# Output products of three layers: tile pairs by seven block products instead of eight, block sums on GpSimd

## The chip, the cores and the metric

One Trainium2 chip, all 8 cores, each with one sequence of the prompt and 16 of the 128 sample sequences. No core talks to another. The metric is the device time of one launch in microseconds, set by the slowest core. The kernel before takes 2015.86 us (median of 3 runs, 2015.81 to 2016.44).

## The reference

A trunk of four layers; each layer normalises its input, projects it, mixes it in three groups of heads, projects the mix back and adds it to the stream:

```
h    = rmsnorm(x, pre_g)
proj = h @ w_in                      # (tokens, 1024) @ (1024, 6400)
u, v, z_a, p, z_b, xc, bg, cg, z_c = split(proj)
a = u * (tril(w_s) @ rmsnorm(v, v_g) + b_s)      # chunks of 128 tokens
b = (pooled mean of p - p) @ w_pg * pool_scale   # windows 2, 4, 8, 16
c = bg * conv3(cg * xc)
mix = concat(a * silu(z_a), b * silu(z_b), c * silu(z_c))   # width 2048
out = mix @ w_out                    # (tokens, 2048) @ (2048, 1024)
x   = x + rmsnorm(out, post_g)
```

The change concerns `out = mix @ w_out` in layers 0, 1 and 2. Layer 3 keeps its form. The next layer's `v` is computed from the new `x` in the same stage, tile by tile.

## The kernel before, in words

A core holds 17 tiles of 128 tokens (tile 16 is the sample group). Activations lie in `big`, 24 slots of 128 channels by 2176 tokens in bf16: 8 slots hold the normalised, transposed input of the current layer (`h0(l)`), 16 hold the mix, and the 8 of the next layer's input are among those 24 in turn. `wout` holds the 16 blocks (128 by 1024) of the layer's output weight in bf16; `ring` holds 8 blocks of input weights, of which `v` takes 6.

For each layer the order is: `b_stage` (pooling), `a_stage` (gating MLP), `c_stage` (convolution), then the output stage, a loop over the tiles in `OUT_ORDER` (16, 0, 1, ... 15). `c_stage` goes over 6 channel blocks; in each it goes over the chunks of tokens in the order 128 (tile 16), 512, 512, 512, 512, and a chunk is four products of 8 matmuls (`mm8`, line 550). At the end of a channel block its four weights are released. That is when GpSimd issues the loads for the slots that came free (lines 481 and 489) and some blocks of `wout` (line 547). At the end of the last channel block of a layer, GpSimd issues the 8 loads of the next `v` weight and two more.

The output stage before, per tile: `out_mm` (line 851) is 16 k-steps by two halves of 512 columns, 32 matmuls into two PSUM banks. `out_ew` squares and sums on ScalarE, `rstd` (line 572) adds epsilon and takes the power -0.5 in two small GpSimd instructions, VectorE scales from PSUM (`stt`) and adds the stream (`tt`), and the tile is stored to `x_mid`. `norm` squares again on ScalarE, uses `rstd` once more, and VectorE writes the next layer's input, which `t_dma` transposes into `big`. Three tiles later `v_mm` multiplies by the `v` weight (16 matmuls) and `v_ew` normalises (ScalarE, `rstd`, VectorE). So a tile needs three `rstd` on GpSimd. Three tiles of `v` are left over at the end of the loop; two of them are placed into the next `b_stage`.

Order: each engine runs its instructions in the order in which they were emitted, and `emit` places the semaphore waits. Where `Plan.on` is set, `emit` collects items instead, and `plan_order` (line 154) then gives out an order: it repeatedly takes the item that could start earliest by the given durations (`dur`) and the dependencies inside the plan, the earlier item on a tie, every engine being free at 0.5. Before, only the start of layer 0 is ordered so; the output stages stand in written order.

## Time and profile before

| | |
|---|---|
| median of 3 runs | 2015.86 us |
| profiled execution, its own time | 2017.03 us |
| its span (slowest core, core 7) | 2015.6 us |
| spans of the 8 cores | 2012.4 to 2015.6 us |
| busy, share of the span | PE 99%, VectorE 54%, ScalarE 29%, GpSimd 18% |
| granted clock of TensorE, mean of the cores | 0.998 to 1.000 of full speed |

"Busy" is the share of the span in which an engine had an instruction under way; loads of matmul weights are counted apart (PEld) and overlap the matmuls. In lists of instructions, "out<-in" are the tiles written and read, and an idle time in brackets is that of the engine before the instruction, with what ended it.

### The profile page before, as it was taken

To read this page: it belongs to the slowest core of one execution; us is meant where nothing else is said; L and a number is where in the kernel's file an instruction comes from. 1 tells how busy PE (TensorE), PEld (TensorE's weight loads), DVE (VectorE), ACT (ScalarE), POOL (GpSimd) and SP (SyncE) were. 2 spreads that over 40 slices of the span, in tenths; PEclk is the share of its full clock that TensorE was granted. 3 is DMA by queue.
4 is the path that set the end of the run, shared out by engine and by line. 5 is a ranking of instruction groups with operands and counts; after the bars stand their busy time and mean duration, and the time that the engine had idled before them with its cause. 6 is when DMAs were issued, how large, how long until landed. Compare 5 with 4: busy or idle time off the path is not lost.

```text
span 2015.6 us, 32819 instructions; the slowest of 8 cores (2012.4 to 2015.6 us)
## 1 busy us (share of the span) xinstructions
PE 1990.4 (99%) x10940; PEld 992.7 (49%) x10940; DVE 1091.0 (54%) x1613; ACT 581.8 (29%) x1127; POOL 367.6 (18%) x701
## 2 busy tenths in 40 slices
PE   6999999999999999999999999999999999999998
PEld 4545554444454554444444555444445455544444
DVE  4675555554575555555457555554545745555433
ACT  4432122223332122223334212222333421222211
POOL 4510011033330001113332001111333100110011
PEclk9999999999999999999999999999999999999999
DMA  8633244384443235518444324443753432353243
GB/s 213 123 58 69 37 89 61 66 199 136 131 84 68 33 63 79 84 29 218 136 121 74 62 43 82 60 74 65 209 134 113 63 76 33 53 81 46 84 147 136
DMA packets 133798, 188.11 MB, mean 93 GB/s; under 512 B 72577, under 2 KB 78977, under 8 KB 133634
## 3 DMA queue, kind: packets, MB, share of 16 engines
q0 software_dynamic: 41040, 71.39, 23.6%
q1 hardware_dynamic: 92450, 114.43, 19.0%
q8 instruction: 92, 1.51, 0.3%
q14 instruction: 72, 0.59, 0.1%
q10 hardware_dynamic: 144, 0.20, 0.0%
HBM read 199.26 MB, written 42.35 MB: 120 GB/s over the span
## 4 chain that ended last, share of the span: by engine, by line
PE 98%; DMA 1%; DVE 0%; issue 0%; POOL 0%; ACT 0%; SPq 0%; POOLq 0%; DVEq 0%; ACTq 0%
PE ps L553 64%; PE ps L855 23%; PE ps L618 9%; PE ps L759 1%; DMA sb_wout<-w_v 1%; PE ps L731 1%; PE ps L890 0%; DMA sb_ar<-x_in 0%; POOL sb_stats L576 0%; DVE sb_hbuf L538 0%; PE ps L602 0%; DVE sb_big L608 0%; ACT sb_hbuf L529 0%; DVE sb_ar L923 0%; DVE sb_big L538 0%
## 5 line engine op out<-in xcount | busy, mean ns | idle before, releaser
L553 PE MATMUL ps<-sb_big,sb_ring 128*128 128x512 bf16 (+2 forms) x7104 | 1327.4, 346 | 3.5 <-DVE sb_big L608 2.2
L553 PEld LDWEIGHTS ps<-sb_big,sb_ring 128*128 128x128 bf16 x7104 | 634.2, 98 | 640.7 <-issue 4.8
L529 ACT ACTIVATE sb_ar<-ps 128x512 f32<-128x512 f32 (+3 forms) x511 | 302.8, 594 | 881.8 <-PE ps L553 549.3
L855 PE MATMUL ps<-sb_wout,sb_big 128*128 128x512 bf16 x2144 | 469.8, 379 | 0.0
L855 PEld LDWEIGHTS ps<-sb_wout,sb_big 128*128 128x128 bf16 x2144 | 209.8, 98 | 248.8
L481 POOL DMA_DIRECT2D sb_ring<-w_t x176 | 94.0, 541 | 925.3 <-PE ps L553 464.2
L534 DVE TENSOR_TENSOR sb_ar<-ps,sb_ar 128x512 f32<-128x512 f32 (+2 forms) x243 | 146.2, 602 | 161.4 <-PE ps L553 157.4
L538 DVE SCALAR_TENSOR_TENSOR sb_ar<-ps,sb_stats,sb_post_bc 128x1024 f32<-128x1024 f32 x67 | 86.0, 1284 | 209.1 <-POOL sb_stats L576 208.5
L538 DVE SCALAR_TENSOR_TENSOR sb_ar<-sb_pcx,sb_convw,sb_ar 128x512 f32<-128x512 f32 (+1 forms) x196 | 145.1, 740 | 88.9 <-ACT sb_ar L815 78.7
L534 DVE TENSOR_TENSOR sb_pcx<-ps,sb_ar 128x512 f32<-128x512 f32 (+1 forms) x98 | 66.7, 681 | 203.8 <-PE ps L553 203.8
L576 POOL TENSOR_TENSOR sb_stats<-sb_stats,sb_neghalf 128x1 f32<-128x1 f32 x203 | 161.0, 793 | 30.1 <-POOL sb_stats L574 0.3
L534 DVE TENSOR_TENSOR sb_big<-sb_ar 128x512 bf16<-128x512 f32 (+2 forms) x242 | 147.4, 609 | 26.0 <-DVE sb_ar L534 0.9
L574 POOL TENSOR_SCALAR sb_stats<-sb_stats 128x1 f32<-128x1 f32 x203 | 52.4, 258 | 513.1 <-ACT sb_ar L529 293.4
L618 PE MATMUL ps<-sb_ring,sb_big 128*128 128x512 bf16 (+1 forms) x816 | 140.4, 326 | 0.0
L815 ACT ACTIVATE sb_ar<-sb_pcx,sb_convw 128x512 f32<-128x512 f32 (+1 forms) x98 | 69.8, 712 | 194.6 <-DVE sb_pcx L534 191.2
L538 DVE SCALAR_TENSOR_TENSOR sb_hbuf<-sb_ar,sb_stats,sb_pre_bc 128x1024 bf16<-128x1024 f32 x53 | 68.1, 1285 | 75.6 <-POOL sb_stats L576 74.2
L618 PEld LDWEIGHTS ps<-sb_ring,sb_big 128*128 128x128 bf16 x816 | 79.7, 98 | 57.2
L534 DVE TENSOR_TENSOR sb_ar<-sb_ar 128x1024 f32<-128x1024 f32 (+4 forms) x91 | 90.8, 997 | 10.1 <-DVE sb_ar L534 0.7
L529 ACT ACTIVATE sb_hbuf<-sb_ar 128x1024 bf16<-128x1024 f32 x53 | 56.0, 1057 | 121.9 <-DVE sb_ar L534 116.0
L538 DVE SCALAR_TENSOR_TENSOR sb_big<-ps,sb_stats,sb_vb_bc 128x768 bf16<-128x768 f32 x64 | 65.1, 1017 | 37.2 <-POOL sb_stats L576 33.2
L529 ACT ACTIVATE sb_big<-ps 128x768 bf16<-128x768 f32 x68 | 55.0, 808 | 83.0 <-PE ps L618 80.6
L534 DVE TENSOR_TENSOR sb_ar<-ps,sb_vb_bc 128x512 f32<-128x512 f32 (+1 forms) x120 | 72.1, 601 | 0.0
(89 smaller groups left out, 636.5 us busy)
## 6 DMA issues: line engine op xcount, KB each, us to landing
sb_ring<-w_t POOLq DMA_DIRECT2D x176, 256.0 KB, 5.3
x_mid<-sb_ar SPq DMA_DIRECT2D x51, 512.0 KB, 2.7
sb_ar<-x_mid SPq DMA_DIRECT2D x51, 512.0 KB, 4.0
sb_wout<-w_out POOLq DMA_DIRECT2D x64, 256.0 KB, 9.0
sb_ar<-x_in SPq DMA_DIRECT2D x20, 512.0 KB, 3.9
y_o<-sb_ar SPq DMA_DIRECT2D x16, 512.0 KB, 2.9
sb_big<-x_in SPq DMA_DIRECT2D x9, 512.0 KB, 9.3
sb_ring<-w_v POOLq DMA_DIRECT2D x24, 192.0 KB, 12.2
```

Source lines behind the costliest of these rows:

```text
L481: emit(POOL, lambda g: g.dma_start(out=flat, in_=a.src), reads=a.gate, writes=a.res, dsem=d_ring[pos], dur=0.58)
L529: return emit(ACT, lambda a: a.activation(out=out, in_=in_, func=func, scale=scale, **kw), reads=reads, writes=writes, dur=0.17 + elems(in ...
L534: return emit(DVE, lambda v: v.tensor_tensor(out=out, in0=in0, in1=in1, op=op), reads=reads, writes=writes, dur=0.15 + elems(out) / 950)
L538: return emit(DVE, lambda v: v.scalar_tensor_tensor(out=out, in0=in0, scalar=scalar, in1=in1, op0=op0, op1=op1), reads=reads, writes=write ...
L553: ins = pe.matmul(bank(b, n), lhsT=wa.ap[:, k, :], rhs=big[:, h0(l) + k, c0:c0 + n], start=(k == 0), stop=(k == 7))
L574: emit(POOL, lambda g: g.tensor_scalar(out=col, in0=col, scalar1=EPS, scalar2=None, op0=ALU.add), reads=[R_stat[si]], writes=[R_stat[si]], ...
L576: emit(POOL, lambda g: g.tensor_tensor(out=col, in0=col, in1=neghalf[:], op=ALU.pow), reads=[R_stat[si], R["neghalf"]], writes=[R_stat[si] ...
L618: ins = pe.matmul(bank(b + bo, n), lhsT=big[:, s0 + k, j * 128:(j + 1) * 128], rhs=wv.ap[:, k, c0:c0 + n], start=(k == 0), stop=(k == 7))
L731: emit(PE, lambda pe: pe.matmul(bank(b, n), lhsT=wpg[:, gi, :], rhs=dd, start=True, stop=True), reads=rm + [R["wpg"]], writes=[bank_res[b]])
L759: ins = pe.matmul(ps[:, 512 * b + jj * 128:512 * b + (jj + 1) * 128], lhsT=big[:, 16 + h, c0 + jj * 128:c0 + (jj + 1) * 128], rhs=wsrc[:, ...
L815: emit(ACT, lambda a_: a_.activation(out=yv, in_=taps[0], func=AF.Copy, scale=cw[:, 0:1]), reads=list(rd) + [R["convw"]], writes=[R_ar[y]] ...
L855: ins = pe.matmul(bank(b + half), lhsT=mix_ap(l, k, j * 128, 128), rhs=wout[:, k, half * 512:(half + 1) * 512], start=(k == 0), stop=(k == ...
```

## The change

The mix of two neighbouring tiles is taken as a 2 by 2 matrix of blocks (tile j or j+1; k-steps 0 to 7 or 8 to 15) and the output weight as another (k-steps; column half). Seven products of 8 matmuls each (56) replace eight (64), by Winograd's form: four sums of mix blocks and four of weight blocks go in, and seven additions put the products together. Three tiles (16, 0, 1) keep the old form, seven pairs (2,3) to (14,15) take the new one.

- `weight_sums`: three sums of weight blocks, each 8 by 512 columns wide, in four GpSimd instructions of 128x1024 bf16, so 12 in a layer. They stand in `c_stage`, after chunks 1, 2 and 3 of the last channel block, ahead of the release of its weights, and write into columns of the layer's input that are no longer read (sum 0 into tiles 0 to 3, sum 1 into tiles 4 to 7, sum 2 into tiles 8 to 11).
- `last_weight_sum`: the fourth, in place in `wout`, on VectorE in four instructions of 128x1024 bf16, after the three single tiles.
- `pair_sums`: four GpSimd instructions of 128x1024 bf16 for each pair, 28 in a layer; those of the first pair are emitted right behind the product of tile 16 and ahead of its `done`.
- `pair_mm`: seven products into banks 0 to 5; a ScalarE copy of 128x512, three VectorE additions of bank and buffer into a buffer (`usum`), four into the bank (`padd`).
- `place`: the order of the 16 blocks in `wout` matches the slots of the mix; `R_wout` has one entry for each half block.
- The output stage of layers 0 to 2 is ordered by `plan_order`. Two of the tiles of `v` come behind the plan, two go into the next `b_stage` as before. The out-stage's temporary is one buffer (8, 9) instead of two in turn.

```diff
+SEVEN = (0, 1, 2)
+LONE = (16, 0, 1)
...
+        def ptt(out, in0, in1, op, reads, writes):
+            return emit(POOL, lambda g: g.tensor_tensor(out=out, in0=in0, in1=in1, op=op),
+                        reads=reads, writes=writes, dur=0.2 + elems(out) / 480)
+
+        def weight_sums(l, i):
+            for k0 in range(0, 8, 2):
...
+                ptt(T_ap(l, i, k0, 2), ins[0], sec[0], ALU.subtract, ins[1] + sec[1], T_res(l, i, k0, 2))
...
                 for ci in (4, 0, 1, 2, 3):
                     c_chunk(l, c, wts, *CHUNKS[ci])
+                    if c == 5 and l in SEVEN and ci in (1, 2, 3):
+                        weight_sums(l, ci - 1)
                 for a in wts:
                     release(a)
...
+        def pair_sums(l, j, S):
+            a11, a12, a21, a22 = A_of(l, 0, j), A_of(l, 1, j), A_of(l, 0, j + 1), A_of(l, 1, j + 1)
+            s1, s2, s4 = (S_of(l, i) for i in S)
+            for o, x, y, op in ((s1, a21, a22, ALU.add), (s2, s1, a11, ALU.subtract), (s4, a12, s2, ALU.subtract),
+                                (a21, a11, a21, ALU.subtract)):
+                ptt(o[0], x[0], y[0], op, x[1] + y[1], o[1])
...
+        def pair_mm(l, j, S, between_):
+            s1, s2, s4 = (S_of(l, i) for i in S)
+            prod(A_of(l, 0, j), B_of(0, 0), 4)
+            act(U_ap[0], bank(4), AF.Copy, reads=[bank_res[4]], writes=[U_res[0]])
+            prod(s2, T_of(l, 1), 5)
+            usum(1, 0, 5)
+            prod(s1, T_of(l, 0), 3)
+            usum(2, 1, 3)
+            prod(s4, B_of(1, 1), 1)
+            padd(1, 2)
+            prod(A_of(l, 1, j), B_of(1, 0), 0)
+            padd(0, 0)
+            between_()
+            prod(A_of(l, 0, j + 1), B_of(0, 1), 4)
+            usum(1, 1, 4)
+            padd(3, 1)
+            prod(A_of(l, 1, j + 1), T_of(l, 2), 2)
+            padd(2, 1)
...
+                for i, j in enumerate(LONE):
+                    b = 2 * (i % 2)
+                    out_mm(l, j, b)
+                    if i == 0:
+                        pair_sums(l, 2, sets[0])
+                        sp_dma(samp[:], sp_in[l + 1], [], [R["samp"]], d_c["samp"])
+                    done(j, b)
+                    x_ahead(i + 4)
+                last_weight_sum()
+                for p in range(7):
+                    j = 2 * p + 2
+
+                    def mid(j=j, p=p):
+                        done(j, 0)
+                        x_ahead(j + 5)
+                        if p < 6:
+                            pair_sums(l, j + 2, sets[p + 1])
+                        next_v()
+                    pair_mm(l, j, sets[p], mid)
+                    done(j + 1, 2)
+                    x_ahead(j + 6)
+                    if p < 6:
+                        next_v()
```

## Rows read from the trace of the kernel before

**Rows 1.** The page: span, busy times, granted clock in 40 slices.
```profile
span 2015.6 us, 32819 instructions; the slowest of 8 cores (2012.4 to 2015.6 us)
...
PE 1990.4 (99%) x10940; PEld 992.7 (49%) x10940; DVE 1091.0 (54%) x1613; ACT 581.8 (29%) x1127; POOL 367.6 (18%) x701
...
PEclk9999999999999999999999999999999999999999
```

**Rows 2.** The page: the chain that ended last, by line.
```profile
PE ps L553 64%; PE ps L855 23%; PE ps L618 9%; PE ps L759 1%; DMA sb_wout<-w_v 1%; PE ps L731 1%; PE ps L890 0%; DMA sb_ar<-x_in 0%; POOL sb_stats L576 0%; DVE sb_hbuf L538 0%; PE ps L602 0%; DVE sb_big L608 0%; ACT sb_hbuf L529 0%; DVE sb_ar L923 0%; DVE sb_big L538 0%
```

**Rows 3.** Chain in order of time, output stage of layer 0: start us, us, what.
```profile
407.81 27.63 PE ps L855 x128
...
438.04 6.91 PE ps L855 x32
444.94 2.60 PE ps L618 x16
...
559.02 5.20 PE ps L618 x32
564.23 3.45 PE ps L553 x16
567.68 2.60 PE ps L618 x16
570.28 2.17 PE ps L553 x16
572.45 2.60 PE ps L618 x16
575.05 3.45 PE ps L553 x16
```

**Rows 4.** Busy time by engine, output stage of layer 0: us, then busy (x instructions).
```profile
407.60:568.00 160.40, 160.40 (x804) 78.57 (x803) 81.98 (x70) 51.86 (x99) 57.00 (x108) 1.00 0.57 155
```

**Rows 5.** Timeline of GpSimd, start of that stage: start us, us, instruction.
```profile
408.66 4.33 POOL L489 DMA_DIRECT2D sb_ring<-w_v  x8 [54.38 <-PE ps L553]
412.92 1.12 POOL L481 DMA_DIRECT2D sb_ring<-w_t  x2
416.15 0.22 POOL L574 TENSOR_SCALAR sb_stats<-sb_stats 128x1 f32<-128x1 f32 x1 [2.11 <-ACT sb_ar L529]
416.52 0.57 POOL L576 TENSOR_TENSOR sb_stats<-sb_stats,sb_neghalf 128x1 f32<-128x1 f32 x1
```

**Rows 6.** GpSimd's instructions, shapes kept apart: xcount, busy us, mean ns.
```profile
L920 POOL TENSOR_TENSOR sb_ar<-sb_ar 128x192 f32<-128x192 f32 x1 | 0.6, 587 | 0.1
...
L905 POOL TENSOR_TENSOR sb_stats<-sb_stats 128x1 f32<-128x1 f32 x1 | 0.2, 189 | 1.1 <-ACT sb_hbuf L529 1.1
```

**Rows 7.** Timeline at 476 us, VectorE and GpSimd.
```profile
476.00 1.28 DVE L538 SCALAR_TENSOR_TENSOR sb_ar<-ps,sb_stats,sb_post_bc 128x1024 f32<-128x1024 f32 x1 [3.01 <-POOL sb_stats L576]
...
477.38 1.23 DVE L534 TENSOR_TENSOR sb_ar<-sb_ar 128x1024 f32<-128x1024 f32 x1
477.64 1.39 POOL L576 TENSOR_TENSOR sb_stats<-sb_stats,sb_neghalf 128x1 f32<-128x1 f32 x1
```

**Rows 8.** VectorE's instructions, shapes kept apart: xcount, busy us, mean ns, idle before.
```profile
L538 DVE SCALAR_TENSOR_TENSOR sb_ar<-sb_pcx,sb_convw,sb_ar 128x512 f32<-128x512 f32 x188 | 141.3, 751 | 88.0 <-ACT sb_ar L815 78.2
L534 DVE TENSOR_TENSOR sb_big<-sb_ar 128x512 bf16<-128x512 f32 x190 | 131.6, 693 | 20.5 <-DVE sb_ar L534 0.9
L534 DVE TENSOR_TENSOR sb_ar<-ps,sb_ar 128x512 f32<-128x512 f32 x190 | 130.7, 688 | 158.4 <-PE ps L553 154.3 <-PE ps L759 4.0
L538 DVE SCALAR_TENSOR_TENSOR sb_ar<-ps,sb_stats,sb_post_bc 128x1024 f32<-128x1024 f32 x67 | 86.0, 1284 | 209.1 <-POOL sb_stats L576 208.5 <-ACT sb_big L529 0.6
L534 DVE TENSOR_TENSOR sb_ar<-sb_ar 128x1024 f32<-128x1024 f32 x67 | 82.2, 1226 | 7.4 <-DVE sb_ar L538 0.5
L538 DVE SCALAR_TENSOR_TENSOR sb_hbuf<-sb_ar,sb_stats,sb_pre_bc 128x1024 bf16<-128x1024 f32 x53 | 68.1, 1285 | 75.6 <-POOL sb_stats L576 74.2 <-POOL sb_stats L574 1.4
L538 DVE SCALAR_TENSOR_TENSOR sb_big<-ps,sb_stats,sb_vb_bc 128x768 bf16<-128x768 f32 x64 | 65.1, 1017 | 37.2 <-POOL sb_stats L576 33.2 <-PE ps L618 4.0
...
L534 DVE TENSOR_TENSOR sb_bdt<-sb_bdt,sb_cstb 128x768 bf16<-128x768 bf16 x4 | 2.2, 551 | 0.0
...
L534 DVE TENSOR_TENSOR sb_ar<-ps,sb_post_bc 128x768 f32<-128x768 f32 x1 | 1.0, 957 | 1.2 <-ACT sb_hbuf L529 1.2
```

**Rows 9.** ScalarE's instructions, shapes kept apart.
```profile
L529 ACT ACTIVATE sb_ar<-ps 128x512 f32<-128x512 f32 x348 | 207.2, 596 | 579.6 <-PE ps L553 527.1 <-DVE sb_big L534 46.0 <-PE ps L731 6.5
L529 ACT ACTIVATE sb_ar<-ps 128x1024 bf16<-128x1024 f32 x67 | 68.5, 1022 | 235.7 <-PE ps L855 235.0 <-POOL sb_stats L574 0.7
...
L529 ACT ACTIVATION_READ_ACCUMULATOR sb_ar<-ps 128x1 f32 x67 | 13.0, 194 | 0.0
```

More of the change, by code:

```diff
@@ L656, in mask_small, with place, wout_piece @@
             tt(bdt[:], bdt[:], m, ALU.mult, [R["bdt"], R["cstb"]], [R["bdt"]])
-        def wout_piece(l, k):
-            pool_dma(wout[:, k, :], w_out[l, k * 128:(k + 1) * 128, :], [R_wout[k]], d_wout[k])
+        def place(l, k):
+            if l not in SEVEN:
+                return k
+            s_ = mslot(l, k)
+            return s_ - 8 + h0(l) if s_ < 16 else s_ - 8
+        def wout_piece(l, kk):
+            k = [place(l, i) for i in range(16)].index(kk)
+            pool_dma(wout[:, kk, :], w_out[l, k * 128:(k + 1) * 128, :], R_wout[2 * kk:2 * kk + 2], d_wout[kk])
@@ new lines, in B_ap, with B_res, T_ap, T_res @@
+        def B_ap(half, ch, k0=0, n=8):
+            return wout[:, 8 * half + k0:8 * half + k0 + n, ch * 512:(ch + 1) * 512]
+        def B_res(half, ch, k0=0, n=8):
+            return [R_wout[2 * (8 * half + k) + ch] for k in range(k0, k0 + n)]
+        def T_ap(l, i, k0=0, n=8):
+            return big[:, h0(l) + k0:h0(l) + k0 + n, i * 512:(i + 1) * 512]
+        def T_res(l, i, k0=0, n=8):
+            return [R_big[h0(l) + k][4 * i + t] for k in range(k0, k0 + n) for t in range(4)]
+        def T_of(l, i):
+            return T_ap(l, i), T_res(l, i)
@@ L661, in b_stage, with last_weight_sum @@
+        def last_weight_sum():
+            for k0 in range(0, 8, 2):
+                tt(B_ap(0, 1, k0, 2), B_ap(1, 1, k0, 2), B_ap(0, 1, k0, 2), ALU.subtract,
+                   B_res(0, 1, k0, 2) + B_res(1, 1, k0, 2), B_res(0, 1, k0, 2))
         def b_stage(l, between):
```

68 lines of the change are left out of this document (63 added, 5 removed).

## The prediction

> **What bounds the kernel now.** I read the page's head first: TensorE has work under way in 99% of the span, at the granted clock 9 tenths or more in every slice, and GpSimd is busy in 18% [rows 1]. Then the chain that ended last: 96% of it is matmuls of lines 553, 855 and 618, and no other engine has more than 1% [rows 2]. So a matmul that goes gives its time back, until something else becomes late. The chain in order of time shows the stage that is changed. One tile's output product is 32 matmuls in 6.91 us (0.216 us each), one tile's `v` product 2.60 us, and they follow each other without a gap [rows 3]. In that stage VectorE is busy 82 of 160 us and GpSimd 57 [rows 4]. The reader should see that TensorE has no slack and that the others have about half, and ask whether the added work fits into that half at each place, not on the mean.
>
> **Matmuls removed.** A pair takes 56 in place of 64: 8 x 0.216 = 1.73 us [rows 3]. With 7 pairs and 3 layers that is 36.3 us, 12.1 in a layer. The `v` products and the weight loads per matmul stay.
>
> **The price of one GpSimd sum.** No row shows one of 128x1024 bf16. The two rows of a plain tensor_tensor on GpSimd give 0.189 us for 1 column and 0.587 for 192 [rows 6], so 2.08 ns a column, and 0.19 + 1023 x 0.00208 = 2.32 us for 1024. Those rows are f32. On VectorE a bf16 sum of 768 columns took 0.551 us against 0.957 for an f32 one out of PSUM [rows 8]; the same factor of 0.58 would give 1.34 us here, which is my lower bound. I take 2.32, since it is from GpSimd itself, and 2.42 with about 0.1 us between instructions, as between the two VectorE instructions at 476.00 and 477.38 [rows 7]. The upper bound is 2.42 plus a wait for VectorE, which comes next.
>
> **GpSimd is held by VectorE.** The power on GpSimd takes 0.57 us by itself [rows 5], but 1.39 us when it starts while VectorE adds two SBUF tiles: it ended at 479.03, 0.42 us after VectorE's end at 478.61 [rows 7]. In two output stages that I went through, all but one of the powers that met this addition were stretched so. The VectorE instructions with two SBUF inputs are the addition of the stream (1.23 us) and the scaling in `norm` (1.29) in each tile, and in a chunk of `c_stage` two of 0.75 and one of 0.69, together 2.2 us [rows 8]. Whether GpSimd's long sums hold VectorE in turn, no row shows: from 0 to 2.3 us for each such instruction. I take little of it and keep the rest as a rival.
>
> The Trainium skill ("SBUF — State Buffer", section "Who interferes with whom") says that VectorE with two SBUF inputs and a GpSimd instruction that reads SBUF exclude each other: whoever comes first keeps the shared port for the whole instruction. By that rule VectorE is held too; the trace agrees for the direction that it shows (0.57 against 1.39 us).
>
> **Start of the output stage.** Let 0 be the end of the last chunk of `c_stage` on TensorE (407.81 in layer 0) [rows 3]. The first weight sum overwrites columns that chunk 0 of the last channel block reads, so it starts when chunk 0 is done, three chunks before 0. A chunk is 32 matmuls, 6.91 us, so at -20.7. GpSimd has nothing to do then (54.38 us idle before 408.66) [rows 5]. The 12 sums take 29.0 us. VectorE has 2.2 us of instructions with two SBUF inputs per chunk, some 7 us over this stretch; GpSimd loses from 0 to 7, I take 5. So the weight sums end at +13.3 (bounds +8.3 and +15.3). Behind them in GpSimd's queue are the eight loads of the `v` weight and two others, 5.4 us from 408.66 to 414.04 [rows 5]: +18.7. Then come the planned items. The planner takes GpSimd as free at 0.5, though it is not, and the first pair's four sums depend on nothing in the plan: at 2.33 + 0.08 each they are set from 0.5 to 10.1. The `rstd` of tile 16 can start by its durations only at about 9.0 (matmuls to 7.4, square and sum 1.2, two hand-overs of 0.2), where the fourth sum is already under way. So all four sums stand ahead of the first `rstd`: +18.7 + 9.7 = +28.4. `rstd` takes 0.9 us (416.15 to 417.09) [rows 5], VectorE's scaling 1.28 [rows 8], with hand-overs +31. Only then are banks 0 and 1 free for tile 1. TensorE has done tiles 16 and 0 by 13.8 and waits for them, 17 us. Without any holding by VectorE it would wait 12. All the matmul time that a layer saves, 12.1 us, goes here already; net +5 us a layer.
>
> In the queue behind are the other `rstd`, and nothing else can go in TensorE's place, since the planner sees that bank free at 12.8 and puts tile 1 next. The `v` weights are issued 13 us later than before; their first use comes 29 us after 0 without the stall, and later with it, so they aren't late.
>
> **The pairs.** TensorE needs 56 x 0.216 + 2 x 2.60 = 17.3 us a pair, against 19.0 for the two tiles before. GpSimd needs four sums, 9.7, and six `rstd` of about 1.0 us with the gap, 6.0, so 15.7 us without being held. VectorE's four instructions with two SBUF inputs are 5.0 us a pair, so from 15.7 to 20.7; since GpSimd is nearly always at work it meets most of them, and I take 0.7 of it: 19.2. VectorE itself: 2 x (1.28 + 1.23 + 1.29 + 1.02) = 9.6 [rows 8], and seven additions of 128x512. Four of these write to PSUM, which no row shows; the nearest is 0.688 for PSUM and SBUF to SBUF, the bounds are 0.6 and 1.3 (half and all of a 1024-column instruction), and I take 0.69: 4.8. With 15 gaps of 0.1 it is 15.9 of 17.3 us. So there is little room: the cover that hid everything before is used up, and GpSimd sets the pace at 19.2. It is 1.9 us a pair above TensorE's need, in six pairs 11, less some 3 us by which GpSimd gets ahead while TensorE does tile 1: +8 us a layer.
>
> **At nothing.** The ScalarE copy (0.6 us a pair [rows 9]; ScalarE is busy a third of the stage [rows 4]). `last_weight_sum`: four bf16 sums, by 0.551 x 1024/768 about 0.73 each, 3 us behind tile 1; its product comes 8.6 us later. Uncovered it would be 3 us a layer. The single temporary: its user comes every 8 us and holds it some 5; if GpSimd is late, it is late by the same wait. The order of `wout` changes no count of loads. SP's loads and stores are the same number, in a planned order, with buffers four tiles deep. At the end of the stage tile 15 has one addition more, 0.7 us, on a chain that had 16.0 us from 559.02 to chunk 3 at 575.05 [rows 3] and needs about 11; a GpSimd that is late by over 4 us there would cost the difference, 0 to 3 us a layer, taken as 0.
>
> **Sum.** In a layer +5 + 8 = +13, in three +39. Against the profiled execution's own 2017.0 (span 2015.6) this is 2056; the median of the runs is 1.2 lower, so 2055 us.
>
> **Rivals.**
> (a) GpSimd's bf16 sums are short, 1.34 us, and the change wins. The weight sums then end about at 0 (the last four can't start before -6.9), the loads at +6.3, the pair's sums at +12, bank 0 is free at +14.6, a stall of 1 us. A pair costs GpSimd 5.8 + 6.0 + at most 5.0 = 16.8 < 17.3. Each layer gains 11, in all 34 us: 1982. For it speaks VectorE's gain in bf16, against it that nothing of the kind is seen on GpSimd. It decides from about 1.8 us a sum down.
> (b) The sums are as long as I take them, but being held costs little, since GpSimd's waits fall where it is idle anyway. The stall of 12 us eats the gain and the pairs run at TensorE's pace: 2016, no change.
> (c) The two engines hold each other. VectorE's 15.9 us a pair get up to 4 waits of some 1.5 us, 22 us a pair: 4.7 over TensorE's need, in six pairs 28 less 3. In `c_stage` VectorE falls behind as well and the stall grows to 20. In a layer +8 + 25 = 33, minus overlap of the two some 3: 2016 + 90 = 2106. For it: both engines are nearly full. By the rule of the Trainium skill named above ("SBUF — State Buffer", "Who interferes with whom") this one would hold; no row bears out the half that decides.
> The fix in (a) could also come from the planned order being other than I worked out (an `rstd` ahead of the sums): then the stall shrinks by up to 9.7 us a layer, and the pairs' pace decides; that lies between (a) and (b).
>
> **Chances.** My forecast 0.44, (a) with its relatives 0.29, (b) 0.09, (c) 0.18. The forecast's own range is 2030 to 2080, from the bounds of the holding. The whole range leaves out the fastest part of (a) (0.09) and the slower half of (c) (0.1): 1982 to 2096. A measurement of this kernel can tell about 0.2% (4 us) from no change. Faster by more 0.29; within it 0.07; slower 0.64.
>
> **What would show it.** GpSimd's sums in the trace: 2.3 us each, longer beside VectorE's additions (steps on price and holding), or 1.3. GpSimd's queue at the start of the stage: weight sums until after the end of `c_stage`, ten loads, four sums, and only then line 574. TensorE idle of 12 to 20 us before the third tile, ended by VectorE's scaling. In the pairs: TensorE idle in each, of 1 to 3 us, and 19 us from pair to pair. The three output stages 163 to 166 us long in place of 151 (plus the last `v` products). If the third tile follows without a gap, the start step is wrong; if the pairs take 17.3 us, the step on the pairs is. The prediction is wrong as a whole if the sums take under 1.8 us.

## The result and the profile after

The changed kernel takes 2082.16 us (median of 4 runs) against 2016.15 us for the kernel before beside it: ratio 1.0321, 95% interval 1.0305 to 1.0336. It is slower by 66 us. The forecast was 2055 us; its own range, 2030 to 2080, ends 2 us below the measured time, and the whole range, 1982 to 2096, holds it. In some of the runs below the cores of one die ran at a lower clock, so beside each time stands the span of a core that was not concerned.

The page of the changed kernel: span, busy time by engine, granted clock and the chain that ended last.

```profile
span 2079.6 us, 32826 instructions; the slowest of 8 cores (2077.2 to 2079.6 us)
...
PE 1970.1 (95%) x10567; PEld 978.2 (47%) x10772; DVE 1262.1 (61%) x1772; ACT 589.5 (28%) x1148; POOL 646.6 (31%) x821
...
PEclk9999999989999999999999999999999999999999
...
PE 79%; POOL 8%; issue 6%; DVE 4%; DMA 2%; ACT 1%; POOLq 0%; DVEq 0%; SPq 0%; ACTq 0%
```

The chain by engine, in the page of the kernel before:

```profile
PE 98%; DMA 1%; DVE 0%; issue 0%; POOL 0%; ACT 0%; SPq 0%; POOLq 0%; DVEq 0%; ACTq 0%
```

TensorE's busy time fell by 20 us, its share of the chain from 98% to 79%, and GpSimd's busy time grew by 279 us. GpSimd has 8% of the chain now and VectorE 4%. The sums' own durations are in the list of GpSimd's instructions (xcount, busy us, mean ns of one, idle before):

```profile
L697 POOL TENSOR_TENSOR sb_big<-sb_big 128x1024 bf16<-128x1024 bf16 x84 | 191.7, 2287 | 17.3 <-PE ps L922 14.9 <-POOL sb_big L697 1.5
...
L697 POOL TENSOR_TENSOR sb_big<-sb_wout,sb_big 128x1024 bf16<-128x1024 bf16 x24 | 58.1, 2455 | 0.0
L697 POOL TENSOR_TENSOR sb_big<-sb_wout 128x1024 bf16<-128x1024 bf16 x12 | 30.1, 2533 | 102.3 <-PE ps L555 102.3
```

The pair sums have a median of 2.12 us (2.10 at the least, 3.11 at the most), where 2.32 was worked out from the f32 rows of 1 and 192 columns [rows 6]. The weight sums have a median of 2.57. The factor of 0.58 that VectorE's bf16 row gave doesn't appear on GpSimd; an f32 sum of this size was not run there.

The start of the output stage of layer 0, GpSimd's timeline (start us, us, instruction, idle before):

```profile
386.81 9.71 POOL L697 TENSOR_TENSOR sb_big<-sb_wout 128x1024 bf16<-128x1024 bf16 x4 [32.97 <-PE ps L555]
396.48 19.38 POOL L697 TENSOR_TENSOR sb_big<-sb_wout,sb_big 128x1024 bf16<-128x1024 bf16 x8
415.80 4.28 POOL L491 DMA_DIRECT2D sb_ring<-w_v  x8
420.00 1.13 POOL L483 DMA_DIRECT2D sb_ring<-w_t  x2
421.06 2.21 POOL L697 TENSOR_TENSOR sb_big<-sb_big 128x1024 bf16<-128x1024 bf16 x1
423.54 2.12 POOL L697 TENSOR_TENSOR sb_big<-sb_big 128x1024 bf16<-128x1024 bf16 x1 [0.26 <-POOL sb_big L697]
425.86 4.20 POOL L697 TENSOR_TENSOR sb_big<-sb_big 128x1024 bf16<-128x1024 bf16 x2 [0.20 <-POOL sb_big L697]
430.15 0.22 POOL L576 TENSOR_SCALAR sb_stats<-sb_stats 128x1 f32<-128x1 f32 x1
```

and TensorE's, in layer 0 and in layer 1:

```profile
407.21 7.07 PE L909 MATMUL ps<-sb_wout,sb_big 128*128 128x512 bf16 x31
418.01 10.00 PE L909 MATMUL ps<-sb_wout,sb_big 128*128 128x512 bf16 x32 [3.73 <-DVE sb_ar L536]
432.87 3.57 PE L909 MATMUL ps<-sb_wout,sb_big 128*128 128x512 bf16 x8 [4.86 <-DVE sb_ar L540]
...
923.52 13.98 PE L909 MATMUL ps<-sb_wout,sb_big 128*128 128x512 bf16 x63
949.71 8.70 PE L909 MATMUL ps<-sb_wout,sb_big 128*128 128x512 bf16 x31 [12.21 <-DVE sb_ar L540]
```

This is the queue that was forecast, in its order: 12 weight sums from -20.4 us (the stage starts at 407.2), ten loads, four sums, and only then the first `rstd`, at +22.9. The third tile's product waits for VectorE's scaling of the first.

The two engines hold each other. That VectorE holds GpSimd shows in the weight sums of `c_stage`, which take 2.57 us where VectorE works beside them and 2.12 otherwise. That GpSimd holds VectorE is in the timeline of VectorE in the last channel block, where GpSimd runs sums without a pause from 386.81 on:

```profile
386.78 5.22 DVE L540 SCALAR_TENSOR_TENSOR sb_ar<-sb_pcx,sb_convw,sb_ar 128x512 f32<-128x512 f32 x2 [0.92 <-ACT sb_ar L867]
...
400.30 1.82 DVE L536 TENSOR_TENSOR sb_big<-sb_ar 128x512 bf16<-128x512 f32 x1
402.05 2.08 DVE L854 COPY sb_pcx<-sb_pcx 128x2 f32<-128x2 f32 x1
404.24 0.69 DVE L536 TENSOR_TENSOR sb_pcx<-ps,sb_ar 128x512 f32<-128x512 f32 x1
```

Two instructions that took 0.75 us each before take 5.22 together, the one of 0.69 us takes 1.82 [rows 8]. The addition that reads PSUM and one SBUF tile keeps its 0.69.

**Where the 64 us are.** The table reads four points of the output stage from TensorE's timeline, in us from the stage's first product, median of the three layers: the start of the second product of the first pair, the end of the last output product, the first product of the next `b_stage`, and the first matmul with `wpg` in it, which all kernels reach behind the same work.

| kernel | time, us | span of a core, us | pairs from | products to | b_stage | wpg |
|---|---|---|---|---|---|---|
| before | 2016.2 | 2015.6 | | 151.4 | 156.4 | 170.7 |
| the change | 2082.2 | 2079.6 | 36.5 | 162.7 | 172.7 | 192.1 |
| planner told, rstd first | 2130.8 | 2097.1 | 24.2 | 166.7 | 179.3 | 197.1 |
| weight sums on VectorE | 2069.8 | 2053.7 | 28.5 | 154.6 | 163.0 | 184.1 |
| no pair sums | 2058.0 | 2026.5 | 27.6 | 145.2 | 155.4 | 174.7 |
| no post-additions | 2075.7 | 2067.1 | 36.4 | 163.7 | 168.7 | 187.9 |
| all sums on VectorE | 2083.6 | 2037.0 | 22.5 | 150.2 | 157.1 | 178.9 |
| pair sums split two and two | 2094.0 | 2064.0 | 29.3 | 156.6 | 169.0 | 187.9 |
| other banks at the end | 2139.1 | 2083.7 | 36.9 | 162.8 | 168.6 | 194.0 |
| five pairs, interleaved | 2036.0 | 2032.1 | 15.8 | 144.4 | 160.7 | 175.0 |
| same, banks and order | 2007.7 | 2006.2 | 15.5 | 146.1 | 153.1 | 167.4 |
| six pairs | 2010.4 | 2008.5 | 15.5 | 144.9 | 152.7 | 168.6 |
| seven pairs in a row | 2066.8 | 2038.5 | 22.5 | 147.0 | 153.2 | 178.4 |
| five pairs, tile sums on GpSimd | 2043.9 | 2039.2 | 15.5 | 158.1 | 165.1 | 179.4 |

The change loses 192.1 - 170.7 = 21.4 us a layer, 64.2 in three, which is the whole difference of the spans (64.0). By TensorE's need it should have gained 12.1, so 33.5 us a layer are to be placed. Start: 36.5 less three tiles (20.7) and a product (1.7), 14.1. Pairs: 126.2 from 36.5 to 162.7, against 116.8 for 48 products of 8 matmuls (83.0) and 13 `v` products (33.8), 9.4. End: 162.7 to 192.1 is 29.4 against 19.3 before, 10.1. In sum 33.6.

### The profile page after: what moved, and what is told of

The parts are those of the page before. It is cut to its first block, busy times and chain, and to the rows that moved or that the text cites. A ratio compares the mean times of both kernels' runs of the same rounds, so it can differ in the third digit from the quotient of the medians.

```text
span 2079.6 us, 32826 instructions; the slowest of 8 cores (2077.2 to 2079.6 us)
## 1 busy us (share of the span) xinstructions
PE 1970.1 (95%) x10567; PEld 978.2 (47%) x10772; DVE 1262.1 (61%) x1772; ACT 589.5 (28%) x1148; POOL 646.6 (31%) x821
## 4 chain that ended last, share of the span: by engine, by line
PE 79%; POOL 8%; issue 6%; DVE 4%; DMA 2%; ACT 1%; POOLq 0%; DVEq 0%; SPq 0%; ACTq 0%
PE ps L555 61%; PE ps L909 6%; PE ps L620 6%; PE ps L922 4%; POOL sb_big L697 4%; POOL sb_stats L578 2%; DVE sb_ar L540 1%; DVE sb_ar L536 1%; PE ps L811 1%; POOL sb_stats L576 1%; PE ps L783 1%; DMA sb_wout<-w_v 1%; POOL sb_ring L491 1%; ACT sb_hbuf L531 1%; DVE sb_big L540 1%
## 5 line engine op out<-in xcount | busy, mean ns | idle before, releaser
L531 ACT ACTIVATE sb_ar<-ps 128x512 f32<-128x512 f32 (+3 forms) x532 | 314.4, 593 | 814.3 <-PE ps L555 531.8
L540 DVE SCALAR_TENSOR_TENSOR sb_ar<-sb_pcx,sb_convw,sb_ar 128x512 f32<-128x512 f32 (+1 forms) x196 | 172.5, 880 | 88.7 <-ACT sb_ar L867 78.5
L909 PE MATMUL ps<-sb_wout,sb_big 128*128 128x512 bf16 x784 | 181.2, 391 | 34.0 <-DVE sb_ar L540 29.3
L697 POOL TENSOR_TENSOR sb_big<-sb_big 128x1024 bf16<-128x1024 bf16 x84 | 191.7, 2287 | 17.3 <-PE ps L922 14.9
L576 POOL TENSOR_SCALAR sb_stats<-sb_stats 128x1 f32<-128x1 f32 x203 | 68.2, 336 | 340.9 <-ACT sb_ar L531 161.0
L536 DVE TENSOR_TENSOR sb_big<-sb_ar 128x512 bf16<-128x512 f32 (+2 forms) x242 | 157.6, 651 | 26.3 <-DVE sb_ar L536 1.4
L922 PE MATMUL ps<-sb_wout,sb_big 128*128 128x512 bf16 x660 | 154.0, 379 | 14.4 <-DVE sb_ar L536 5.8
L578 POOL TENSOR_TENSOR sb_stats<-sb_stats,sb_neghalf 128x1 f32<-128x1 f32 x203 | 145.4, 717 | 29.2 <-POOL sb_stats L576 0.2
L909 PEld LDWEIGHTS ps<-sb_wout,sb_big 128*128 128x128 bf16 x800 | 80.0, 100 | 134.6 <-issue 45.9
L922 PE MATMUL ps<-sb_big 128*128 128x512 bf16 x492 | 114.0, 379 | 4.7 <-DVE sb_ar L540 3.6
L540 DVE SCALAR_TENSOR_TENSOR sb_hbuf<-sb_ar,sb_stats,sb_pre_bc 128x1024 bf16<-128x1024 f32 x53 | 77.9, 1470 | 59.2 <-POOL sb_stats L578 57.9
L922 PEld LDWEIGHTS ps<-sb_wout,sb_big 128*128 128x128 bf16 x672 | 64.3, 98 | 94.1 <-issue 23.0
```

The source lines that it names most:

```text
L531: return emit(ACT, lambda a: a.activation(out=out, in_=in_, func=func, scale=scale, **kw), reads=reads, writes=writes, dur=0.17 + elems(in ...
L536: return emit(DVE, lambda v: v.tensor_tensor(out=out, in0=in0, in1=in1, op=op), reads=reads, writes=writes, dur=0.15 + elems(out) / 950)
L540: return emit(DVE, lambda v: v.scalar_tensor_tensor(out=out, in0=in0, scalar=scalar, in1=in1, op0=op0, op1=op1), reads=reads, writes=write ...
L576: emit(POOL, lambda g: g.tensor_scalar(out=col, in0=col, scalar1=EPS, scalar2=None, op0=ALU.add), reads=[R_stat[si]], writes=[R_stat[si]], ...
L578: emit(POOL, lambda g: g.tensor_tensor(out=col, in0=col, in1=neghalf[:], op=ALU.pow), reads=[R_stat[si], R["neghalf"]], writes=[R_stat[si] ...
L697: return emit(POOL, lambda g: g.tensor_tensor(out=out, in0=in0, in1=in1, op=op), reads=reads, writes=writes, dur=0.2 + elems(out) / 480)
```

## The experiments

**The order at the start.** The planner is told when GpSimd is free, and the first pair's sums come behind the first tile's `rstd`.

```diff
-                s = max(ready, free.get(id(q), 0.5))
+                s = max(ready, free.get(id(q), Plan.late.get(id(q), 0.5)))
...
+                Plan.late = {id(POOL): 14.0}
...
                     if i == 0:
-                        pair_sums(l, 2, sets[0])
                         sp_dma(samp[:], sp_in[l + 1], [], [R["samp"]], d_c["samp"])
                     done(j, b)
+                    if i == 0:
+                        pair_sums(l, 2, sets[0])
```

> The change, but the planner is told that GpSimd is free only at 14 us, and the first pair's four sums are emitted behind the first tile's rstd, not ahead of it. In the change the third tile begins 25.2 us after the end of c_stage and TensorE waits 12.2 us for it. Theory Q (GpSimd's total work and the mutual holding with VectorE set the pace of the whole stage): the wait before the third tile falls from 12 us to about 3, but the four sums are then late for the first pair and the time is given back; the stage gets 0 to 3 us shorter, in all 2072 to 2082 us. Rival O (a wrong order at one place costs its own time and nothing else): 9 us a layer less, 2055 us.

Measured: 2130.8 us, span 2097.1. The pairs begin 12.3 us earlier in the stage, and the stage is still 5 us longer. Both expectations are too low; that the time is given back is theory Q's direction. One place where it is given back can be seen on TensorE in layer 0:

```profile
431.91 1.89 PE L923 MATMUL ps<-sb_big 128*128 128x512 bf16 x8
441.03 3.36 PE L621 MATMUL ps<-sb_ring,sb_big 128*128 128x512 bf16 x10 [7.23 <-issue]
```

No engine releases the first `v` product at 441.03. Its weights were not late: the last of them landed at 435.96, 5 us before. What landed last is the transposed copy of tile 16 that the product reads: issued at 431.29, landed at 440.01, 1.0 us before the product. In layer 1 it is the same: the weights at 955.40, the copy at 960.32, the product at 961.33 after a wait of 3.34 us. The copy took 8.7 us in layer 0, where 2.8 is usual; the ten loads moved beside it, which is a likely reason and was not tested. Why the pairs are slower too (142.5 us in place of 126.2) is not settled.

**Weight sums on VectorE.**

```diff
-                ptt(T_ap(l, i, k0, 2), ins[0], sec[0], ALU.subtract, ...
+                tt(T_ap(l, i, k0, 2), ins[0], sec[0], ALU.subtract, ...
```

> The change with its 12 weight sums a layer on VectorE in place of GpSimd. GpSimd then has nothing in c_stage; VectorE gets 12 bf16 instructions of 0.68 us (last_weight_sum's unhindered duration), 9.4 us with gaps, where it had 8.4 us idle in three chunks. Theory Q: the loads of the v weight go out at once, the first pair's sums end at +14, the third tile's wait falls to 2 or 3 us; the pairs keep their pace of 18.7 us (12.4 us above TensorE's need in 7 pairs): each layer gets 10 us shorter, 2050 us. Rival V (VectorE's load is what limits, GpSimd's is not): VectorE is late by what it takes on, gain under 4 us a layer, 2070 us or more.

Measured: span 2053.7 (2069.8 as timed). 26 us in all less than the change, 8.1 a layer at `wpg`; of this the start has 8.0, and the pairs keep their pace (126.1 against 126.2). Theory Q. In `c_stage` four such sums that took 9.71 us on GpSimd take 2.49 on VectorE.

**No pair sums**: the four sums of each pair are left out, so the tiles' outputs are not the reference's.

```diff
-                ptt(o[0], x[0], y[0], op, x[1] + y[1], o[1])
+                pass
```

> The change without its four pair sums a pair on GpSimd (the products take what lies in the buffers; the weight sums stay). Theory Q: with 28 x 2.2 us a layer gone, nothing holds VectorE in the pairs, they run at TensorE's 17.3 us (118.5 us for seven pairs with their v products in place of 130.9), the third tile starts 9 us earlier, and the end of the stage loses its 7 us: about 25 us a layer less, 2005 us. Rival V (VectorE's seven additions a pair set the pace): only the 9 us at the start go, the pairs stay at 18.7: 2053 us.

Measured: span 2026.5; 17.4 us a layer less. The pairs run in 117.6 us, 0.8 over TensorE's need, as theory Q has it, so the seven additions a pair on VectorE, without the sums, hold up nothing in the pairs. The total is neither's, 2005 nor 2053: the end costs what it did in the change, 29.5 us, which neither expected. With theory Q's 7 us less there it would have been about 2005. So the end's cost doesn't come from GpSimd's pair sums.

**No post-additions**: the seven additions of a pair are left out (the products stay uncombined).

```diff
-            tt(U_ap[o], U_ap[a], bank(b), ALU.add, [U_res[a], bank_res[b]], [U_res[o]])
+            pass
...
-            tt(bank(b), bank(b), U_ap[a], ALU.add, [bank_res[b], U_res[a]], [bank_res[b]])
+            pass
```

> The change without the seven additions of 128x512 a pair on VectorE (the products stay uncombined). Theory Q (GpSimd's queue with its holding sets the pace, VectorE is full besides): VectorE has 5.5 us a pair less, meets GpSimd's sums with the same four instructions, and GpSimd's need of 15.7 us plus holds stays: the pairs get a third to a half of their 12.4 us back, the start keeps its 13.8 us: 5 us a layer, 2065 us. Rival V: the pairs run at TensorE's pace and the end of the stage is in time, 19 us a layer less, 2025 us.

Measured: span 2067.1, near the 2065 of theory Q, but from another place. The stage is 4.2 us a layer shorter. The pairs took 127.3 us, 1.1 more than with the additions; the end took 5.2 less (24.2 in place of 29.4). So relieving VectorE buys nothing in the pairs while the GpSimd sums are there. The busy times of the stretch of the pairs, from a window of each kernel (us, then busy PE, PEld, DVE, ACT, POOL), first the change:

```profile
443.80:570.00 126.20, 118.27 (x581) 56.70 (x591) 102.13 (x103) 44.80 (x86) 90.70 (x101) 1.00 0.47 140
```

then the one without post-additions:

```profile
442.90:570.00 127.10, 117.35 (x582) 57.11 (x592) 84.69 (x60) 45.75 (x90) 97.44 (x103) 1.00 0.53 144
```

Neither engine is full: VectorE 81% and GpSimd 72% in the change, 67% and 77% without the additions. Theory Q was right that the loss hangs on the sums, but not by its sum of durations. What TensorE waits for in the pairs are PSUM banks, as in these rows of the change:

```profile
469.66 2.76 PE L620 MATMUL ps<-sb_ring,sb_big 128*128 128x512 bf16 x16 [1.00 <-DVE sb_big L540]
...
479.75 1.89 PE L922 MATMUL ps<-sb_wout,sb_big 128*128 128x512 bf16 x8 [2.15 <-DVE sb_ar L536]
```

A bank goes back through ScalarE, `rstd` on GpSimd and VectorE. With a 2.1 us sum ahead of `rstd` and one more hold on VectorE, that chain can be longer than the two or three products that TensorE has in the meantime. This is a reading of the rows: no run changes the chain's length alone.

**All sums on VectorE.**

```diff
-                ptt(T_ap(l, i, k0, 2), ins[0], sec[0], ALU.subtract, ins[1] + sec[1], T_res(l, i, k0, 2))
+                tt(T_ap(l, i, k0, 2), ins[0], sec[0], ALU.subtract, ins[1] + sec[1], T_res(l, i, k0, 2))
...
-                ptt(o[0], x[0], y[0], op, x[1] + y[1], o[1])
+                tt(o[0], x[0], y[0], op, x[1] + y[1], o[1])
```

> The change with all its sums, of weights and of tiles, on VectorE; GpSimd has the small rstd instructions and its loads alone, as before the change. Theory Q (GpSimd's queue of 2.1 us sums sets the pace, and holding between the two engines makes it worse): no long GpSimd instruction is left; VectorE's need per pair is 15.9 + 4 x 0.78 = 19.0 us, 1.7 above TensorE's; no wait at the start; the end stays at 10 us and the next b_stage at 19.4: some 5 us a layer above the kernel before, 2031 us. Rival V (VectorE's load was the limit already): it gets 12.5 us of sums a layer in c_stage and 22 in the pairs on top, and the time rises above the 2080 of the change.

Measured: span 2037.0, as theory Q (2031) more than rival V. The start is as good as free (22.5 is three tiles and a product). The pairs take 127.7 us, no better than in the change: VectorE is busy 107 of 127.6 us of them. That its own queue now returns the banks late is what this suggests; no run shows it by itself.

**Pair sums split two and two**, with the weight sums on VectorE as well.

```diff
-                ptt(T_ap(l, i, k0, 2), ins[0], sec[0], ALU.subtract, ins[1] + sec[1], T_res(l, i, k0, 2))
+                tt(T_ap(l, i, k0, 2), ins[0], sec[0], ALU.subtract, ins[1] + sec[1], T_res(l, i, k0, 2))
...
-                ptt(o[0], x[0], y[0], op, x[1] + y[1], o[1])
+                (tt if o is s4 or o is a21 else ptt)(o[0], x[0], y[0], op, x[1] + y[1], o[1])
```

> The weight sums on VectorE; of the four sums of a pair two on VectorE (the third and the one in place), two on GpSimd. By needs without holding: VectorE 17.5 us, GpSimd 10.4, TensorE 17.3 a pair. Theory Q: what holding is left comes from two GpSimd sums a pair and costs under 1 us each; pairs near 18 us, no long wait at the start, the end as in the change: 2020 to 2030 us, faster than all sums on VectorE. Rival H (holding by any long GpSimd sum is dear, since VectorE is full): slower than all on VectorE, 2035 to 2050.

Measured: span 2064.0, slower than all on VectorE by 27 us and beyond rival H's upper end. By loads it was the best balanced kernel. The pairs are alike (127.3 us against 127.7); of the 27 us the start has 6.8 a layer and the end 2.6. At the start GpSimd has the four sums of the first two pairs in its queue, from 413.82 to 423.4, and the first `rstd` comes behind them at 423.49. So what the split costs is again a place in GpSimd's queue at the start, not the pace of the pairs.

**Other banks at the end.**

```diff
-                st["bank"] = 0
-                vjob(vq[0])
                 st["bank"] = 4
+                vjob(vq[0])
+                st["bank"] = 0
                 vjob(vq[1])
...
+                def first(j=vq[2]):
+                    st["bank"] = 4
+                    vjob(j)
...
                 def fin(j=vq[3], l=l):
+                    st["bank"] = 0
                     vjob(j)
```

> The change with other PSUM banks for the four v products behind the plan: the first gets banks 4 and 5 (free early), the second 0 and 1, the third 4 and 5, the fourth 0 and 1; in the change the first waits 3.2 us for the scaling of tile 14 out of banks 0 and 1, and the third 3.5 us for the first one's banks. Theory B (the wait is for the bank alone): both waits go, with them most of the lowered clock behind them: 6 to 8 us a layer, 2060 us. Rival C (the last two tiles end 3.5 us apart instead of 9.5, and their elementwise work is late whatever the bank): the waits move to the next product that needs a bank or a transposed tile, 2075 to 2080.

Measured: span 2083.7, rival C (2075 to 2080, a little more). The first wait shrinks from 3.2 to 0.6 us and the third `v` product waits 7.8 instead of 3.5:

```profile
572.16 2.76 PE L620 MATMUL ps<-sb_ring,sb_big 128*128 128x512 bf16 x15 [0.57 <-DVE sb_ar L540]
574.76 3.62 PE L555 MATMUL ps<-sb_big,sb_ring 128*128 128x512 bf16 x16
586.17 4.97 PE L620 MATMUL ps<-sb_ring,sb_big 128*128 128x512 bf16 x16 [7.79 <-DVE sb_big L540]
```

But the third `v` product again gets the banks of the first, now 4 and 5, and waits until VectorE has released them. So the run moves the wait and doesn't answer whether banks of its own for each leftover `v` product would remove it.

**Five pairs between single tiles.** All sums on VectorE. The fourth weight sum goes into freed columns of the layer's input and into `samp`, so that single tiles can still use the whole weight; its product is then 16 matmuls of 256 columns.

```diff
+UNITS = ((16,), (0,), (1, 2), (3,), (4, 5), (6,), (7, 8), (9,), (10, 11), (12,), (13, 14), (15,))
...
+                    if len(u) == 1:
...
+                        out_mm(l, u[0], b)
+                        done(u[0], b)
...
+                    else:
+                        pair_mm(l, u[0], S3, lambda j=u[0]: done(j, 0))
```

> Five pairs instead of seven, each between single tiles: 16, 0, (1,2), 3, (4,5), 6, (7,8), 9, (10,11), 12, (13,14), 15. All sums on VectorE; the fourth weight sum gets a place of its own, so that single tiles can follow pairs. TensorE's need falls by 5 x 1.73 = 8.6 us a layer against the kernel before. Theory Q: with no long GpSimd instruction, what counts is whether VectorE fits; a pair and a single tile need 19.0 + 5.3 of TensorE's 26.8 us, so it fits, the last tile stands alone as before and the end costs what it did before: 26 us gained, 1990 us, up to 2000 if the start is late by VectorE's weight sums. Rival C (products of a pair end too close together for its elementwise chain, wherever it stands): each pair costs its 1.7 us gain again, 2016 us or more.

Measured: 2036.0, span 2032.1. By the total it is rival C (2016 or more). By the products it is nearer to theory Q: they end at 144.4, 7.0 us earlier than in the kernel before, where theory Q had 8.6. But the end costs 30.6 us (144.4 to 175.0), though a single tile is the last unit. There the next 32 `v` matmuls wait 5.3 us and take 7.56, where 5.36 is usual:

```profile
549.32 2.76 PE L620 MATMUL ps<-sb_ring,sb_big 128*128 128x512 bf16 x15
557.38 7.56 PE L620 MATMUL ps<-sb_ring,sb_big 128*128 128x512 bf16 x32 [5.29 <-DVE sb_big L540]
```

The two `v` products in a row both use banks 6 and 7. That, tile 0's bank, and a VectorE sum that waited 4.4 us for a store were mended next.

**The same with banks and order mended**, and **six pairs**.

```diff
-                        v_mm(l + 1, v, 6)
-                        v_ew(l + 1, v, 6)
+                        vb = 4 if nv[0] == 14 else 6
+                        v_mm(l + 1, v, vb)
+                        v_ew(l + 1, v, vb)
...
-                        b = 2 if ui == 1 else 0
+                        b = 6 if ui == 1 else 0
                         out_mm(l, u[0], b)
+                        if ui == 0:
+                            pair_sums(l, pairs_left.pop(0)[0], S3)
                         done(u[0], b)
                         if ui == 0:
                             last_weight_sum(l)
-                            pair_sums(l, pairs_left.pop(0)[0], S3)
...
-                st["bank"] = 4
+                st["bank"] = 2
                 vjob(vq[0])
+                st["bank"] = 6
```

Six pairs differ from it in one line:

```diff
+UNITS = ((16,), (0,), (1, 2), (3, 4), (5,), (6, 7), (8, 9), (10,), (11, 12), (13, 14), (15,))
```

> The interleaved kernel with five pairs, and three places mended that its trace showed idle: the last planned v product and the one behind the plan get banks 4, 5 and 2, 3 in place of 6, 7 and 4, 5 (a 5.3 us wait, and the halved clock behind it); tile 0 gets banks 6 and 7 in place of 2 and 3, which the first pair's second product waited for (1.5 to 5.3 us); and the part of the fourth weight sum that waits 4.4 us for a store stands behind the first pair's sums on VectorE, not ahead of them. Theory Q: with no idle stretch left TensorE's own need decides, 8.6 us a layer under the kernel before: 1990 us, 1998 if the end stays 2 us late. Rival C (pairs bring VectorE's chain late wherever they stand): the waits move on, 2015 or more.

> The same with six pairs: 16, 0, (1,2), (3,4), 5, (6,7), (8,9), 10, (11,12), (13,14), 15. TensorE's need is 10.4 us a layer under the kernel before. Two pairs and a single tile need 2 x 19.0 + 5.3 = 43.3 us of VectorE against 2 x 17.3 + 9.5 = 44.1 of TensorE. Theory Q: it just fits, 1985 us, or VectorE is late where two pairs follow each other (one set of buffers for the tile sums, 1 to 2 us each) and it comes out level with five pairs, 1988 to 1996. Rival C: 2020 us or more.

Measured with five pairs: 2007.7 us, ratio to the kernel before 0.9955, interval 0.9942 to 0.9969: faster than both kernels, by 0.45% over the one before. It lies between theory Q (1990) and rival C (2015), with a third of the gain of theory Q. The end costs 21.3 us in place of 30.6, by banks and order alone. `wpg` is reached at 167.4 in place of 170.7, so 3.3 us a layer are kept of 8.6; the rest is in short waits, among them one in front of the first product of the next `b_stage`:

```profile
560.40 3.61 PE L555 MATMUL ps<-sb_big,sb_ring 128*128 128x512 bf16 x16 [1.77 <-DVE sb_big L540]
```

With six pairs it is 2010.4 us (0.9973, 0.9961 to 0.9984), outside both expectations and 2.7 us slower than five. Its waits in layer 0 are 0.9 us each at the `v` products at the end of the first and the second pair, 1.2 behind the last pair and 2.6 in front of `b_stage`; where the middle pairs meet there is none. So it isn't shown that pairs in a row are what costs the 2.7 us.

**Seven pairs in a row**, else as in the five-pair kernel, but for the banks of the single tiles and of the first leftover `v` product.

```diff
+UNITS = ((16,), (0,), (1,)) + tuple((j, j + 1) for j in range(2, 16, 2))
...
-                        b = 6 if ui == 1 else 0
+                        b = (0, 6, 2)[ui]
...
-                st["bank"] = 2
+                st["bank"] = 0
                 vjob(vq[0])
```

> The last five-pair kernel, 2007.7 us, with the tiles in the order of the change: 16, 0, 1 alone, then seven pairs with no single tile between them. All sums on VectorE, the fourth weight sum in its place of its own. Theory L (each pair hands its elementwise work to engines that must give PSUM banks back within two or three products; a single tile after each pair is what lets them): with VectorE 84% busy the pairs run 1.6 us over TensorE's need as they did with all sums on VectorE, and the last two tiles end close together: 2030 to 2038 us. Rival N (what helped was the banks and the order of the weight sums, and more pairs are better): 12.1 us a layer less matmul time, 1995 to 2002 us.

Measured: span 2038.5, half a microsecond above theory L's upper end. The products end at 147.0, hardly later than with five pairs, but the end costs 31.4 us (147.0 to 178.4) against 21.3, with one wait of 7.5 to 7.9 us in each layer. In layer 0 it is the wait of tile 14's `v` product, which was given banks 0 and 1, held by tile 13's until 571.05. Its other input, tile 14's transposed copy, had landed at 565.71, so of the 7.9 us about 5.3 go to the bank and 2.4 to the tile. Whether a pair as the last unit costs the 10 us, or the banks do, this run doesn't separate; with a single tile last and unlucky banks the end had cost 30.6.

**Five pairs with the tile sums on GpSimd.** (In the five-pair kernel `ptt` issues on VectorE.)

```diff
-                ptt(o[0], x[0], y[0], op, x[1] + y[1], o[1])
+                emit(POOL, lambda g, o=o, x=x, y=y, op=op: g.tensor_tensor(out=o[0], in0=x[0], in1=y[0], op=op),
+                     reads=x[1] + y[1], writes=o[1], dur=0.2 + elems(o[0]) / 480)
```

> The last five-pair kernel, 2007.7 us, with its four tile sums a pair back on GpSimd (the weight sums stay on VectorE). In the 26.8 us of a pair and a single tile GpSimd then has 4 x 2.2 + 9 x 1.0 = 17.8 us, VectorE 3.1 less than its 24. So by load both have more room than in any kernel of the study but the one before. Theory H (what is dear is the small rstd behind a 2.1 us sum and the holding of VectorE, not the load): the banks come back late after each pair, 2 to 4 us each, and the first pair's sums are late behind the loads of the v weight: 2025 to 2050 us. Rival Load (room by the sums of durations is enough): at or below 2007 us.

Measured: 2043.9 us (1.0132, 1.0112 to 1.0152), theory H: 36 us slower than with the same sums on VectorE, though VectorE has 20 bf16 instructions a layer less. One window over the same 119 us of layer 0 (columns as above), first the sums on VectorE:

```profile
430.00:549.00 119.00, 116.69 (x629) 60.79 (x627) 93.32 (x103) 43.37 (x86) 43.21 (x80) 1.00 0.57 161
```

then on GpSimd:

```profile
430.00:549.00 119.00, 109.23 (x572) 55.50 (x570) 87.44 (x83) 38.38 (x75) 75.02 (x87) 0.99 0.54 154
```

VectorE at 73% and GpSimd at 63% keep TensorE waiting; VectorE at 78% and GpSimd at 36% do not. Nothing else differs between the two kernels, so the busy share doesn't decide. The longest waits stand in the first two units with sums, 1.5, 2.5 and 2.9 us:

```profile
433.92 2.76 PE L620 MATMUL ps<-sb_ring,sb_big 128*128 128x512 bf16 x16 [1.50 <-DVE sb_ar L536]
...
441.31 7.07 PE L930 MATMUL ps<-sb_wout,sb_big 128*128 128x512 bf16 x32 [2.46 <-DVE sb_ar L540]
...
457.32 5.30 PE L943 MATMUL ps<-sb_wout,sb_big 128*128 128x512 bf16 x16 [2.89 <-DVE sb_ar L540]
```

More than half of the 12 us that the pairs lose in layer 0 is there, where the first sums stand behind the ten loads; each wait behind is 0.3 to 1.9 us, less than the 2 to 4 that were expected after every pair.

## Why the prediction was right, and where it was off

The direction and the main mechanism were right: the change is slower, because GpSimd's sums stand in the way of its short instructions. The size was nearly right partly by luck. Without the end, which the sum left out, the terms as measured would give about 2051 us; the end, 30 us in all, carried the time out of the forecast's own range.

**Matmuls removed, 12.1 us a layer: right.** With nothing in the way the pairs take 117.6 us (no pair sums) against a need of 116.8.

**The price of one sum, 2.32 us: right in kind**, 2.12 measured, and rival (a), 1.34 us by analogy with VectorE's bf16, was wrong. An operation's own f32 rows on the same engine were the better ground than another engine's gain.

**The start, 17 us: right in mechanism, measured 14.1.** Weight sums ended at +8.6 us (forecast +13.3), the loads at +13.8 (18.7), the four sums at +22.9 (28.4). GpSimd lost about 4 us to holding there, where 5 was taken: nine of the 12 weight sums took 2.57 us and not 2.12. The rest of the difference is the sum itself, which is shorter. In layers 1 and 2 the stall is one wait of 12.2 us before the third tile, the 12 that the prediction gave without any holding, and about 2 us because that tile then takes 8.70 us at a granted clock of 0.81; a slower clock after a wait was no term of the prediction. Only in layer 0 is it different: the row of 3.73 us at the second tile is TensorE waiting for a bank of `c_stage` that VectorE reached late. Rival (c) had this, the forecast did not. Moving only the weight sums away gave back 8.0 us a layer, at this place.

**The pairs, +8 us: right size (9.4), reason in part wrong.** The step set GpSimd's need, 15.7 to 20.7 us a pair, against TensorE's 17.3, as if the fuller engine gave the pace, and had 19.2 us from pair to pair. Measured are 18.3, with waits of 0.3 to 2.2 us, with GpSimd at 72 to 77% and VectorE at 67 to 81%. Without the sums the loss is gone; without VectorE's additions it stays; with the sums on VectorE it stays too. With sums on VectorE and single tiles in between it is nearly gone, and with the same sums on GpSimd it is back, though VectorE has less to do then. That the length of the chain that returns a bank counts, and not the load, fits all of these, but is argued and not shown by a run of its own.

**The end, taken as 0 with 3 us as its bound: this term was wrong.** It measured 10.1 us a layer, 30 of the 66. The step compared one tile's chain, 11 us, with 16.0 us of room. It left out that the last additions complete tiles 14 and 15 only 2.3 us apart (at 568.5 and 570.8 in layer 0), where the products of the last two tiles ended 9.5 us apart before. So two chains stand in the queues of VectorE and ScalarE at once. ScalarE takes its work in the written order, and the leftover `v` products wait behind it. TensorE in layer 0:

```profile
573.17 7.04 PE L620 MATMUL ps<-sb_ring,sb_big 128*128 128x512 bf16 x31 [3.17 <-DVE sb_ar L540]
...
587.18 4.44 PE L620 MATMUL ps<-sb_ring,sb_big 128*128 128x512 bf16 x16 [3.52 <-DVE sb_big L540]
```

and ScalarE, the norm of the last tile and behind it the square of the first of these `v` products, whose matmuls had been done for over 5 us:

```profile
581.72 1.06 ACT L531 ACTIVATE sb_hbuf<-sb_ar 128x1024 bf16<-128x1024 f32 x1 [5.18 <-DVE sb_ar L536]
...
582.78 0.79 ACT L531 ACTIVATE sb_big<-ps 128x768 bf16<-128x768 f32 x1
```

The third `v` product waits for the banks of the first. The end costs 21.3 us with five pairs and mended banks, and 29 to 31 in the change, without pair sums, with five pairs before the mending, and with seven pairs in a row. So banks and order alone can make a difference of that size (9.3 us), and how much of the 10.1 the last pair itself makes is open. The change also left one `v` product more behind the plan than the kernels from the interleaved one on. Elementwise work of the leftover `v` products ahead of the last tile's norm, or banks of their own for all of them, was not tried with seven pairs.

**Rival (c), mutual holding: its mechanism is real** (5.22 us for two instructions of 0.75), and the measured time lies between my forecast, 27 us below, and its 2106, 24 above. Its price was too high: in the pairs most instructions of VectorE with two SBUF inputs found the port free or nearly so, 1.35 us in the mean for the stream's addition in place of 1.23. The rule of the Trainium skill ("SBUF — State Buffer", section "Who interferes with whom") is borne out in the direction too that the trace of before did not show.

**Rival (b) and the loads at nothing.** The stall did eat the gain, as (b) said, but the pairs did not run at TensorE's pace. The `v` weights were not late, as the prediction had it: in the change they landed at +29.6 us, ahead of their first use, and even with the stall shortened they were there 5 us early. What came late there was the transposed copy of tile 16.

## What to carry to other kernels

Where an engine in the middle of a chain that frees a buffer has short instructions, look at what stands ahead of each of them, not only at the engine's load. Here sums of 2.1 us ahead of one short `rstd` made the stall at the start, and the busy shares didn't tell which kernel waits. When work is saved by pairing tiles, the results come in bursts: look at the last pair and the stage that follows it, and give the products left over there banks that are free and elementwise work that doesn't stand behind the last tile's. Before giving elementwise bf16 work to GpSimd because VectorE is half busy, price it on VectorE: here it took a third of the time there.
